# Six raw places and eight split places instead of eight and seven, in a two-block transformer kernel

## The reference

```python
h = rmsnorm(x, g_norm)
z = jnp.einsum('bsd,dn->bsn', h, w_in)          # n = 13312
...                                             # diff, dilated and memory attention
merged = gates[:, :, 0] * y_a + gates[:, :, 1] * y_b + gates[:, :, 2] * y_m
return x + jnp.einsum('bsd,de->bse', merged, w_out)
```

```python
mod = c_act @ ada_w[i] + ada_b[i]               # 1024 x 6144 for each layer
h = modulate(rmsnorm_2(x, norm_gain[i, 0]), sh1, sc1)
x = x + g1[:, None, :] * mixer(h)
h = modulate(rmsnorm_2(x, norm_gain[i, 1]), sh2, sc2)
x = x + g2[:, None, :] * swiglu(h, ffn_w_gu[i], ffn_w_down[i])   # hidden width 2816
```

## Time and profile before

| | |
|---|---|
| median of 3 runs | 2190.66 us (2187.43 to 2190.84) |
| profiled execution | 2190.97 us, its span 2189.2 us |
| TensorE, VectorE, ScalarE, GpSimd busy | 98%, 72%, 49%, 9% of the span |
| mean granted clock of TensorE | 0.995 |
| DMA | 472.47 MB, 216 GB/s over the span |

### The profile page before, as it was taken

The page is one execution under the profiler, slowest core; times in us unless marked ns, Lnnn a source line. Parts: engine busy times, 40 slices in busy tenths (PEclk is TensorE's granted clock), DMA queues, the critical chain, the costliest instruction groups (busy, mean ns, idle before and its releaser), DMA issues. The chain is left out here.

```text
span 2189.2 us, 34066 instructions
## 1 busy us (share of the span) xinstructions
PE 2134.9 (98%) x13639; PEld 1901.4 (87%) x13639; DVE 1566.8 (72%) x2164; ACT 1081.5 (49%) x2091; POOL 190.1 (9%) x242
## 2 busy tenths in 40 slices
PE   8999999999999999999999998999999999999998
PEld 6999888889988888778999787999898999778997
DVE  6578657766776677667898677899745896657545
ACT  5454555544545565455445543454555454465433
POOL 1101001101010011010001001001000001110000
PEclk9999999999999999999999999999999999999999
DMA  9888645577786455633999434799644797535561
GB/s 303 289 267 245 220 149 159 171 236 228 253 269 206 139 169 178 222 126 124 314 348 350 165 122 144 237 361 361 229 136 145 243 358 245 167 100 180 196 204 75
DMA packets 297284, 472.47 MB, mean 216 GB/s; under 512 B 20241, under 2 KB 153051, under 8 KB 297126
## 3 DMA queue, kind: packets, MB, share of 16 engines
q1 hardware_dynamic: 286566, 440.68, 60.1%
q0 software_dynamic: 10560, 29.61, 4.5%
HBM read 465.36 MB, written 4.85 MB: 215 GB/s over the span
## 5 line engine op out<-in xcount | busy, mean ns | idle before, releaser
L150 DVE TENSOR_TENSOR wlo<-raw,whi 128x1024 fp32r<-128x1024 f32 x640 | 770.5, 1234 | 206.0 <-ACT whi L144 205.0
L144 ACT ACTIVATE whi<-raw 128x1024 fp32r<-128x1024 f32 x640 | 645.5, 1056 | 162.3 <-DMA raw<-in_ffn_w_gu 72.4
L138 PE MATMUL G<-HTh,whi 128*128 128x256 f32 x2336 | 671.2, 287 | 9.6 <-ACT pool L144 7.0
L138 PE MATMUL G<-HTh,wlo 128*128 128x256 f32 x2336 | 661.5, 283 | 0.0
L138 PE MATMUL G<-HTl,whi 128*128 128x256 f32 x2336 | 661.4, 283 | 0.0
L138 PEld LDWEIGHTS G<-HTh,whi 128*128 128x128 f32 x2336 | 448.2, 192 | 18.6 <-issue 10.6
L138 PEld LDWEIGHTS G<-HTl,whi 128*128 128x128 f32 x2336 | 448.4, 192 | 2.1
L138 PEld LDWEIGHTS G<-HTh,wlo 128*128 128x128 f32 x2336 | 448.2, 192 | 0.0
L144 ACT ACTIVATE pool<-G 128x128 f32<-128x128 f32 (+2 forms) x400 | 165.4, 434 | 518.0 <-PE G L138 465.0
L138 PE MATMUL G<-whi,HTh 128*128 128x512 f32 (+1 forms) x784 | 311.8, 398 | 5.7 <-ACT HTh L144 4.9
L138 PE MATMUL G<-whi,HTl 128*128 128x512 f32 (+1 forms) x784 | 303.0, 386 | 6.1 <-DVE HTl L158 6.1
(11 more groups left out here) (194 smaller groups left out, 2258.1 us busy)
## 6 DMA issues: line engine op xcount, KB each, us to landing
raw<-in_ada_w SPq DMA_DIRECT2D x192, 512.0 KB, 6.3
raw<-in_ffn_w_gu SPq DMA_DIRECT2D x352, 256.0 KB, 5.1
raw<-in_w_in SPq DMA_DIRECT2D x128, 512.0 KB, 4.6
raw<-in_ffn_w_down SPq DMA_DIRECT2D x88, 512.0 KB, 7.2
raw<-in_w_in SPq DMA_DIRECT2D x160, 256.0 KB, 4.6
raw<-in_swa_w_in SPq DMA_DIRECT2D x24, 512.0 KB, 4.8
pool<-mod_rows POOLq DMA_DIRECT2D x24, 512.0 KB, 6.2
raw<-in_gla_w_in SPq DMA_DIRECT2D x24, 512.0 KB, 5.0
```

The source lines that it names most:

```text
L138: return self.e.matmul(out, a, b, start=start, stop=stop, skip_group_check=True) if self.e else self
L144: return self.e.activation(out, a, func, bias=bias, scale=scale, accum_out=accum) if self.e else self
L150: return self.e.tensor_tensor(out, a, b, op) if self.e else self
```

## The change

Two constants. `raw` goes from 8 to 6 places of 4 KB per partition; `whi` and `wlo` go from 7 to 8 places of 4 KB each. All loops, engines and instructions stay; what is fetched when, which place a piece gets, and what the planner decides follow from the constants.

```diff
-NRAW = 8
-NSPL = 7
+NRAW = 6
+NSPL = 8
 LOOK = 4
```

## The result

The changed kernel takes 2242.46 us (median of 4 runs, 2238.22 to 2245.02) against 2190.75 us (median of 4, 2187.43 to 2191.15) for the kernel before: ratio 1.0237, 95% interval 1.0225 to 1.0248. It is 2.4% slower, 51.7 us. The forecast was 2196.2 us with a range to 2205.

What follows compares the result with a forecast made beforehand. TensorE was taken as the bound, busy 2134.9 of 2189.2 us. The profiled 2190.97 + 2.2 + 0.1 (turns) + 3.2 (third feed-forward stage) = 2196.5, against the median 2196.2 us; range 2189 to 2205.

Steps and rivals of the forecast that it cites:

- One: the split places: Turns between layers: one more subtraction ahead of the norm costs +2.2 us in layers 0 and 3, +0.1 in layer 1.
- Two, third stage: Third feed-forward stage: six raw places make loads late, 0.8 us in each of 4.2 groups, +3.2 us.
- Two, first two stages: First two feed-forward stages: late loads are covered by VectorE's idle time and the reserve, so 0.
- the reserve of 4.4 us: First two feed-forward stages: time between a piece's subtraction and its first product never falls below 4.4 us.
- Three, the planner's order: Attention stages: a reshuffled instruction order can win or lose, bounded at 2 us either way, taken as 0.
- the 15 forced pieces of 832: Dilated-attention stages of both first layers: fetches forcing out what is six instead of eight places old, 15 of 832.
- That the raw places cost nothing: Rival: the load queue empties and only the turns cost, 2193.0 us; chance 0.33.
- The loads lose in all three stages: Rival: the DMA queue is at its limit in the feed-forward stages, 9 us more, 2205 us; chance 0.12.

Runs made afterwards that it cites:

- e1: Kernel before with six raw places instead of eight, counted and real, and seven split places as before: 2241.54 us, ratio 1.0234.
- e2: Kernel before with only six real raw places, while the planner still counts eight; seven split places: 2217.56 us, ratio 1.0124.
- e10: The changed kernel's places (six raw, eight split) under the order the planner writes for eight raw places: 2217.03 us, ratio 1.0112.
- e5: Changed kernel with the planner reckoning a load to land 3.0 us after its place comes free, not 4.5: 2231.06 us, ratio 1.0193.
- e8: As e2, with two modulation-row loads at the feed-forward stage ends of layers 0 to 2 cut from 1024 to 128 columns: 2215.38 us, ratio 1.0119.
- e11: As e3 (planner forces pieces at six places), but its landing estimate looks at the release eight pieces back: 2190.19 us, ratio 1.000.
- e7: Kernel before with seven raw places, counted and real, and seven split places: 2191.00 us, ratio 1.0011.
- e9: As e2, with half of each column piece left unloaded from the first feed-forward stage on: 2193.33 us, ratio 1.0015.
- e6: As e3, with the planner reckoning a load to land 3.0 us after its place comes free, not 4.5: 2210.24 us, ratio 1.0094.
- e4: Kernel before with ten raw places instead of eight and six split places instead of seven: 2200.22 us, ratio 1.005.
- e3: Kernel before with the planner counting six raw places while eight exist; seven split places: 2212.94 us, ratio 1.0108.

## Why the prediction was wrong

**One: the split places, +2.3 us at the turns. Right in each place.** The transposes in layers 0 and 3 wait 1.43 us (forecast about 1.4); the exits wait 1.68 and 0.79 (forecast 1.7 and 0.8); the end of the first block 1.63 and 0.94. Without the eighth split place (e1) they are 0.29, 0.54 and 1.92 as before. In the delay of first products, the turn in layer 0 costs the changed kernel 1.0 us and e1 nothing. In total time e1 against the changed kernel, and e2 against e10, show nothing above their intervals.

**Two, third stage, +3.2 us. Right in mechanism, near in size:** from piece 504 to 528 the delay grows by 2.6 us in the changed kernel (51.8 to 54.4) and by 2.5 in e2 (20.0 to 22.5), though by 5.0 to 5.2 in e5, e8 and e10, which have six places too. TensorE's own waits for the low half are 1.6 us there, less than the "several" foretold.

**Two, first two stages, "0": this step failed.** The lateness had been found and sized rightly, 0.8 to 1.4 us per group of 17.5 us: the measured deficit of 0.1 us a piece is 1.1 us in a group's 11.6 pieces. What failed is the cover set against it. VectorE's idle time of 1.6 us a group was taken as time in which it can make good a late load, but it cannot subtract what has not landed. It became more idle, not less. The other cover, the reserve of 4.4 us, was real and is spent in four to six groups, of nine. The sum was at hand in the prediction ("18 groups at 1.0 us less two reserves of 4.4 would be 9 us"); with the chance of 0.12 it went to a rival. Even that rival was too cheap: e2 lost 10.1 us from piece 304 to 352 (3.6 to 13.7) and 10.2 from 392 to 448 (9.8 to 20.0), some 20 in place of 9, because the last group blocks ScalarE's evacuations behind its late splits (a gap of 5.77 us in e2) and the clock falls after it (0.77 in that window of the changed kernel).

**Three, the planner's order, "2 us either way and take 0": this step failed too, by about 23 us.** The prediction counted the 15 forced pieces of 832, and they indeed cost nothing (e11). The half sentence "its estimate of landings also changes a little" held the loss. It was dismissed by the size of the edit, and not followed through the plan: whether the subtraction of a piece comes before or after the last product ahead of its own is decided by it, and one such case costs evacuation, split and subtraction in series, 3.38 us, and then the clock. The bound was drawn from TensorE's present waits in these stages, but what a new order can cost is not bounded by the waits of the old one.

**The clock: it has no term in the sum.** Every lost microsecond was counted once, as a gap. By the mean granted clocks above, some 14 of the 51.7 us are products at the lower clock behind the new gaps, on top of the gaps.

**The rivals.** That the raw places cost nothing fails with six places; with seven the time is that of before (e7), but not for the reason given: issue to landing is hardly shorter (6.80 against 6.88 us), and the reserve carries. "The loads lose in all three stages" is the half that belongs to the places. How near the queue is to a limit with eight places: the transfers of the kernel before from 1100 to 1180 us of its span, by slices of 2 us and in all.

```profile
GB/s 389 373 400 399 316 278 230 290 368 386 376 396 396 310 329 351 345 368 375 393 397 385 278 266 371 394 368 369 372 399 384 245 341 388 371 365 372 385 397 369
DMA packets 18413, 28.57 MB, mean 357 GB/s; under 512 B 1189, under 2 KB 10427, under 8 KB 18406
```

The Trainium skill ("DMA: Bandwidth & Descriptors", Specifications) gives about 358 GB/s as a core's share of HBM; the trace's mean of 357 is of that size, but the first four slices, 8 us, average 390. So the figure is not shown to be a ceiling for this core, and the rival's premise, a queue at that limit, does not hold as it stands.

The places cost before the bandwidth does: six places moved 325 GB/s in the first stage (e2), less than the 338 that the same queue moved with eight, and lost. e9 lost nothing there up to piece 344, at 260; it takes bytes and flight away together, so it does not tell those two apart:

```profile
1043.00:1207.00 164.00, 156.15 (x1114) 146.89 (x1113) 141.40 (x174) 72.95 (x158) 14.15 (x13) 1.00 0.95 325
```

```profile
1041.00:1205.00 164.00, 161.41 (x1155) 152.94 (x1155) 145.28 (x180) 76.28 (x164) 16.00 (x14) 0.99 0.81 260
```

Not tried: the changed kernel's order with the evacuations written ahead of the splits at the stage ends, so the share of that blocking in the 10 us is read from the trace and not measured by itself. Nor is it shown why e5 and e6 win back 9 us after their new stall.

## What to carry to other kernels

A ring of buffers carries a stage while places times the pace of use is longer than the time from issue to release. If it is shorter, each piece comes late by the difference over the places, and the reserve pays for that until it is gone. Work both out from issue, landing and release before a place is given up. Here 6 x 1.51 = 9.1 us against 9.6 was a loss, and 7 x 1.51 = 10.6 against 10.8 fell short by less than the reserve held. The time needed is itself not the same for each number of places (9.6 us with six, 10.8 with seven), so a place more or less is best measured. Idle time of the engine that consumes late data is no cover; only data that is already there is. Where one number is both a buffer count and an input of a scheduler, price the two apart, and follow the new order through the queues of the engines that work in order.

## What the runs showed of the hardware

- A stall of TensorE costs more than its gap. The changed kernel lost 35.2 us to idle time and another 18.7 us to longer busy time, some 14 of them by the granted clock. Around the gap of 5.71 us there were 6.2 us of idle time and 3.2 us of slower products; in windows around the gaps the granted clock was 0.86 and 0.77. Shorter gaps do it at times. The exits of the first two feed-forward stages in the kernel before have one gap of 1.92 us each, alike in length, and the granted clock of the window around is 0.81 at the one and 1.00 at the other:

```profile
1222.00:1231.00 9.00, 7.08 (x26) 5.69 (x27) 6.55 (x11) 2.06 (x6) 1.42 (x3) 0.81 0.36 117
1566.00:1575.00 9.00, 7.01 (x32) 5.20 (x32) 7.22 (x13) 3.74 (x9) 1.64 (x3) 1.00 0.45 145
```

- The flight of a load is no constant of its size. From 1060 to 1180 us of the span, 512 KB of column piece took a median of 7.2 us from issue to landing in the kernel before and 6.1 in e2, 256 KB in e9 4.3. The number of places alone does not set it: the same view has 7.2 us with seven places (e7), 6.7 with ten (e4), and 6.3 with eight under the six-place order (e3). What is shorter with seven places is the time from landing to release, 4.0 us against 5.2 (from the table: 10.79 - 6.80 and 12.05 - 6.88).
